# First MLP group of a hybrid decoder step: normalised a block per tile, up-projection weights in the slots free first, squares on ScalarE

## The reference, cut to what matters

```python
h   = rms_norm(x) * (1 + sc1) + sh1
proj = h @ w_in                       # q | f | i | g | B | C | h
# HGRN2 heads: gated recurrence over chunks of 64, per-head RMSNorm, SiLU gate
# short conv: y = B * causal_depthwise_conv3(C * h)
x   = x + g1 * (concat([o_rec, o_conv]) @ w_out)
h2  = rms_norm(x) * (1 + sc2) + sh2
x   = x + g2 * (square(relu(h2 @ w_up)) @ w_down)      # D_FF = 4096
y   = rms_norm(x) * g_final
```

## Time and profile before

| | |
|---|---|
| time, median of 3 runs | 898.47 us (895.25 to 898.91) |
| the profiled execution, its time | 894.26 us |
| its span on the slowest core (0) | 892.7 us |
| spans of the eight cores | 883.8 to 892.7 us |
| mean granted TensorE clock | 0.978 to 0.986 |
| TensorE, VectorE, ScalarE, GpSimd busy | 92, 54, 40, 19% |
| DMA | 106.71 MB, mean 120 GB/s |

### The profile page before, as it was taken

How to read it: one execution, slowest core, us unless ns; L and a number is a source line. 1 busy time by engine, 2 the same in 40 slices (tenths; PEclk the granted TensorE clock), 3 DMA queues, 4 the chain that set the end, 5 groups by cost and what they waited for, 6 DMA issues and landing times.

```text
span 892.7 us, 16990 instructions; the slowest of 8 cores (883.8 to 892.7 us)
## 1 busy us (share of the span) xinstructions
PE 825.2 (92%) x6005; PEld 521.0 (58%) x6005; DVE 482.7 (54%) x902; ACT 361.1 (40%) x771; POOL 173.4 (19%) x231
## 2 busy tenths in 40 slices
PE   1488899999999999876999999999999999999996
PEld 1356687677775776734544654465456545654864
DVE  1365797577777867771551764256335634542422
ACT  3266874546667666612401532233123312311412
POOL 3110134344115235200002101100210111011002
PEclk9888999999999999989999999999999999999999
DMA  8999914958995243999993513122222113102001
GB/s 154 193 193 195 200 45 98 193 171 173 205 206 139 96 142 72 189 167 173 187 210 109 194 52 115 48 95 71 95 84 71 60 48 118 36 13 89 30 2 48
DMA packets 27727, 106.71 MB, mean 120 GB/s; under 512 B 3798, under 2 KB 4822, under 8 KB 22652
## 3 DMA queue, kind: packets, MB, share of 16 engines
q0 software_dynamic: 6624, 44.14, 29.6%
q1 hardware_dynamic: 19292, 55.46, 18.3%
q10 hardware_dynamic: 1728, 6.03, 2.1%
HBM read 123.93 MB, written 22.68 MB: 164 GB/s over the span
## 4 chain that ended last, share of the span: by engine, by line
PE 81%; DMA 7%; issue 4%; DVE 4%; ACT 3%; POOL 0%; DVEq 0%; ACTq 0%; POOLq 0%; SPq 0%
PE B L484 79%; DMA xn<-x 4%; DMA xe<-xp 3%; PE B L495 2%; ACT W L511 2%; DVE W L522 1%; DMA cB<-constB 0%; DVE W L518 0%; DVE Sd L518 0%; DVE W L528 0%; ACT A L511 0%; DVE mix L518 0%; DVE hT L524 0%; DVE W L532 0%; ACT WX L511 0%
## 5 line engine op out<-in xcount | busy, mean ns | idle before, releaser
L484 PE MATMUL B<-h2T,wup 128*128 128x384 bf16 (+1 forms) x1536 | 242.2, 319 | 9.0 <-DVE uT L518 6.9
L484 PE MATMUL B<-wdn,uT 128*128 128x512 bf16 (+1 forms) x1120 | 237.5, 373 | 0.0
L511 ACT ACTIVATE W<-B 128x384 f32<-128x384 f32 (+2 forms) x241 | 119.0, 496 | 231.7 <-PE B L484 206.6
L484 PEld LDWEIGHTS B<-h2T,wup 128*128 128x128 bf16 x1536 | 150.2, 98 | 95.5 <-issue 12.2
L484 PE MATMUL B<-hT,win 128*128 128x256 bf16 (+1 forms) x1728 | 199.8, 273 | 6.5 <-DMA win<-w_in 4.8
L484 PEld LDWEIGHTS B<-hT,win 128*128 128x128 bf16 x1728 | 162.1, 100 | 32.3 <-issue 7.3
L484 PEld LDWEIGHTS B<-wdn,uT 128*128 128x128 bf16 x1120 | 109.0, 98 | 121.9
L518 DVE TENSOR_TENSOR uT<-W,B 128x384 bf16<-128x384 f32 (+1 forms) x192 | 100.5, 530 | 108.8 <-ACT W L511 87.8
L518 POOL TENSOR_TENSOR xr<-xr,W 128x512 f32<-128x512 f32 x63 | 82.6, 1312 | 284.4 <-DVE W L518 264.1
L518 DVE TENSOR_TENSOR W<-B,Gp 128x512 f32<-128x512 f32 (+1 forms) x65 | 44.0, 679 | 106.2 <-PE B L484 103.5
L484 PE MATMUL B<-wout,mix 128*128 128x512 bf16 x272 | 64.9, 390 | 9.1 <-DVE mix L518 7.0
(11 more groups left out here) (150 smaller groups left out, 643.7 us busy)
## 6 DMA issues: line engine op xcount, KB each, us to landing
x<-xr SPq DMA_DIRECT2D x17, 512.0 KB, 5.9
xn<-x SPq DMA_DIRECT2D x17, 512.0 KB, 4.4
xr<-x SPq DMA_DIRECT2D x17, 512.0 KB, 3.4
ada<-w_ada POOLq DMA_DIRECT2D x8, 1024.0 KB, 16.4
xr<-xp SPq DMA_DIRECT2D x16, 512.0 KB, 7.6
wdn<-w_down POOLq DMA_DIRECT2D x8, 1024.0 KB, 35.3
wup<-w_up POOLq DMA_DIRECT2D x8, 1024.0 KB, 22.3
yp<-xr SPq DMA_DIRECT2D x15, 512.0 KB, 2.6
```

Of the source, the lines that this page charges most:

```text
L484: ins = e.matmul(o_, lhsT=l_, rhs=r_, start=st, stop=sp_, skip_group_check=True)
L511: return P.op("act", lambda e: e.activation(out=out, in_=in_, func=func, **kw), r, w, c, prio=prio)
```

## The change

Seven things change together.

1. Group 0 is [0, 1, SAMPLE] in place of [SAMPLE, 0, 1]. Its blocks are normalised one at a time, at step H of prompt tiles 4, 5 and 6 (`n_` 5 to 7), in place of all three at step B of the last tile. h2T0 gets a layout with the block outermost (its right-hand side in `up` is three pieces of 128 columns) and moves to the place of Gs. The sample block's modulation uses its own xn buffer as scratch.
2. The class N of banks (transposes of norms) is served in the order of the code (FIFO).
3. The first two blocks of group 1 are fetched at step F of the last tile (`got`); group 1 is normalised after 12 of the 32 chains of group 0's `up`.
4. The weight slots are dealt anew: wup0 and wup1 get the region that wdn0 and wdn1 had and stand at the same place of GpSimd's queue; wup2 to 7 follow the order in which the last tile frees `win`; UPORD and upos go. wdn2 to 7 wait for the mixer's last TensorE operation.
5. In group 0's `up` both operations are on ScalarE: relu from the bank into the bank, then its square into uT. VectorE takes no part. Later groups stay as they were.
6. Gs can't be loaded before group 0's `up` has read h2T0; Gs and g_final are loaded after it. The 16 state steps, whose buffers overlap Gs, stay in group 1.
7. The prompt's conv state is stored from uc (128 pieces of 32 bytes) and no longer from uco (512 pieces of 8 bytes). Tile to mix slot follows a list, since slot 2 now overlaps h2T0.

```diff
-    FIFO = "PXU"
+    FIFO = "PXUN"
...
-    for j, off in enumerate((u0, u0 + 8192, u0 + 16384, a0 - 8192, a0 + 24576, a0 + 32768, a0 + 40960, a0 + 49152)):
+    for j, off in enumerate((4 * 8192, u0 + 16384, 7 * 8192, 8 * 8192, a0 + 24576, a0 + 32768, a0 + 40960, a0 + 49152)):
...
+    for j, off in enumerate((u0, u0 + 8192, 8192, 2 * 8192, 0, 3 * 8192, 5 * 8192, 6 * 8192)):
+        t, rg = place("wup%d" % j, [128, 8, 512], BF16, offset=off)
...
-    h2T0, _ = place("h2T0", [128, 8, 384], BF16, offset=m0)
+    h2T0, _ = place("h2T0", [128, 3, 8, 128], BF16, offset=xG + 4096)
...
-        mi = state["mixi"] % 3
+        mi = (0, 1, 2, 0, 1, 0, 2, 1, 0)[state["mixi"]]
...
+            if pre == "h2T0_":
+                act(bank[:, 0:N], bank[:, 0:N], AF.Relu, [bn], [bn])
+                act(uT[:, fc, 0:N], bank[:, 0:N], AF.Square, [bn], ["uT%d" % fc])
+                continue
             W, Wn = WB.take()
             act(W[:, 0:N], bank[:, 0:N], AF.Relu, [bn], [Wn])
-            tt("dve", uT[:, upos[fc], 0:N], W[:, 0:N], bank[:, 0:N], ALU.mult, [Wn, bn], ["uT%d" % fc])
+            tt("dve", uT[:, fc, 0:N], W[:, 0:N], bank[:, 0:N], ALU.mult, [Wn, bn], ["uT%d" % fc])
...
-    bgroups = [[SAMPLE, 0, 1], [2, 3, 4], [5, 6, 7], [8, 9, 10], [11, 12, 13], [14, 15]]
+    bgroups = [[0, 1, SAMPLE], [2, 3, 4], [5, 6, 7], [8, 9, 10], [11, 12, 13], [14, 15]]
...
+            if step == "H" and n_ in (5, 6, 7):
+                norm2(bgroups[0][n_ - 5:n_ - 4], None, "h2T0_", n_ - 5)
+            if step == "F" and n_ + 1 == len(tiles):
+                got = [fetch2(blk) for blk in bgroups[1][:2]]
             if step == "B" and n_ + 1 == len(tiles):
-                WB = View(wall[2:6])
-                for j in UPORD[:7]:
+                for j in range(2, 8):
                     load_up(j)
-                norm2(bgroups[0], h2T0, "h2T0_")
-        if n_ == 6:
-            load_dn(0); load_dn(1)
+                load_dn(0)
+                load_dn(1)
+        if n_ == 5:
+            load_up(0); load_up(1)
+    mixed = [[o for o in P.ops if o.eng == "pe"][-1]]
+    for j in range(2, 8):
+        load_dn(j, mixed)
...
+            up(bl, None, "h2T0_", 0, 12)
+            norm2(bgroups[1], h2T, "h2T", 0, got)
+            up(bl, None, "h2T0_", 12, 32)
+            load_gates(1, prompt=False)
```

More of the change, by code:

```diff
@@ L600, in assemble @@
         P.buf("wout%d" % j, rg); wout.append(t); wout_n.append("wout%d" % j)
[L601 to L604, removed]
     a0 = at["p"]
@@ L639, in assemble @@
     uT, _ = place("uT", [128, 32, 384], BF16, offset=a0)
-    for i, fc in enumerate([4 * b + i for b in UPORD for i in range(4)]):
-        P.buf("uT%d" % fc, (a0 + i * 768, a0 + (i + 1) * 768))
-    upos = {fc: i for i, fc in enumerate([4 * b + i for b in UPORD for i in range(4)])}
+    for fc in range(32):
+        P.buf("uT%d" % fc, (a0 + fc * 768, a0 + (fc + 1) * 768))
     u0 = at["p"]
@@ L680, in assemble @@
     SR = Ring("S", 2, [128, 512], F32, offset=xG + 4096)
+    h2T0, _ = place("h2T0", [128, 3, 8, 128], BF16, offset=xG + 4096)
+    for s in range(3):
+        P.buf("h2T0_%d" % s, (xG + 4096 + s * 2048, xG + 6144 + s * 2048))
     xeR = Ring("xe", 2, [128, 1024], F32, offset=xG)
-    SbF = (one("rout", [128, 512], F32, offset=xG + 4096), "rout")
+    SbF = (one("rout", [128, 512], F32, offset=xG + 8192 + 2048), "rout")
     sg2R = Ring("sx", 2, [128, 512], F32, offset=xG + 4096)
@@ L736, in load_up, with load_dn @@
         dma("pool", flat(wup[j]), wup_d[j], [], [wup_n[j]], MB2)
-    def load_dn(j):
-        dma("pool", flat(wdn[j]), wdn_d[j], [], [wdn_n[j]], MB2)
+    def load_dn(j, after=()):
+        dma("pool", flat(wdn[j]), wdn_d[j], [], [wdn_n[j]], MB2, after=after)
     P.buf("cBm", P.bufs["cB"].rng, "cB")
@@ L1123, in mixer_tile @@
                    [csn, nH], [ubn])
[L1124 to L1127, removed]
+                copy("pool", uc[:, ccs[0]:ccs[0] + 2, :], uv[:, :, 256:258], [ubn], [ucn])
                 for i, cc in enumerate(ccs):
@@ L1179, in mixer_tile, with fetch2, norm2 @@
             dma("sp", x1_d[xblk + b], xr[:], [xrn], ["x1_%d" % (xblk + b)], 128 * 4096)
-    def norm2(blocks, h2T, pre):
-        for s, blk in enumerate(blocks):
-            nbv, nbn = normed(None, None, fetch(x1_d[blk], ["x1_%d" % blk], None, "sp"))
+    def fetch2(blk):
+        return fetch(x1_d[blk], ["x1_%d" % blk], None, "sp")
+    def norm2(blocks, h2T, pre, s0=0, got=()):
+        for i, blk in enumerate(blocks):
+            s = s0 + i
+            x = got[i] if i < len(got) else fetch2(blk)
+            nbv, nbn = normed(None, None, x)
+            dst = h2T0[:, s, :, :] if pre == "h2T0_" else h2T[:, :, s * 128:(s + 1) * 128]
             if blk == SAMPLE:
-                sample_mod(nbv, nbn, h2T, pre + "%d" % s, s * 128, 16, 24)
+                sample_mod(nbv, nbn, dst, pre + "%d" % s, 0, 16, 24, x)
                 continue
@@ L1228, in part @@
             bank, bn = banks[(s, dh)]
-            mm([(bank[:, :], uT[:, upos[a * 8 + k], s * 128:(s + 1) * 128], wdn[dh * 4 + a][:, k, :], a == 0 and k == 0, a == 3 and k == 7)
+            mm([(bank[:, :], uT[:, a * 8 + k, s * 128:(s + 1) * 128], wdn[dh * 4 + a][:, k, :], a == 0 and k == 0, a == 3 and k == 7)
                 for k in range(8)], ["uT%d" % (a * 8 + k) for k in range(8)] + [wdn_n[dh * 4 + a]], [bn])
@@ L1258, in finish @@
                 for a in range(4):
-                    mm([(bank[:, 0:c1 - c0], uT[:, upos[a * 8 + k], s * 128:(s + 1) * 128], wdn[dh * 4 + a][:, k, h0:h0 + c1 - c0],
+                    mm([(bank[:, 0:c1 - c0], uT[:, a * 8 + k, s * 128:(s + 1) * 128], wdn[dh * 4 + a][:, k, h0:h0 + c1 - c0],
                          a == 0 and k == 0, a == 3 and k == 7) for k in range(8)],
```

49 lines of the change are left out of this document (26 added, 23 removed).

## The result

The changed kernel took 884.14 us (median of four runs, 883.08 to 886.49), the kernel before 898.47 us beside it. The ratio is 0.9853, with a 95% interval of 0.9832 to 0.9875: 13.2 us faster by the ratio and 14.3 by the medians, where 16.4 were forecast. One more set of runs on another chip gave 886.28 us and a ratio of 0.9828 (0.9798 to 0.9858). Now and then an execution is some per cent longer at a lower clock on some cores; the medians here leave such slow runs out, as the ratios do.

What follows compares the result with a forecast made beforehand. The prediction took TensorE, busy 92% of the span, as the bound. Gaps and slow clock of 19.4 us less costs of 2, 0, 1 and 0 gave 16.4 us, so 882 us from a median of 898.47; range 875 to 893 us.

Steps and rivals of the forecast that it cites:

- The gaps and the slow clock: End of mixer and first up-projection: three TensorE gaps, 14.6 us, and slow clock, 2.45 and 2.3 us, all gained.
- the first two gaps: TensorE waits before the last tile's output projection, 5.59 us, and before the first up-projection, 2.19 us; both would go.
- the third: TensorE gap of 6.86 us in the middle of the first up-projection, traced to a late xn load; would go.
- Term (1): Normalising the first group in prompt tiles 4 to 6 costs the mixer 2 us, bounds minus 2 to 15.7.
- Rival D: Mixer, 280 to 350 us: ScalarE stands on late next-tile x loads, five waits of 5.7 us; 910 us; chance 0.07.
- Term (2): First up-projection: ScalarE's relu and square take 1.0 to 1.15 us a pair, TensorE stays the bound; cost 0.
- Term (3): Weight loads on POOL's queue: last lands near 463 us, TensorE asks at 463.9; level, cost 1 us.
- Term (4): Gs, loadable only after h2T0 is read, lands near 458 us; cover 17 us, cost 0, up to +3.
- wup0 at the projection: Sign of being right: wup0's matmuls begin within 1 us of the last hT projection, near 377 us.
- the first up without a gap: Sign of being right: the first group's up-projection has no gap of over 1 us.
- Clock 1.00 in each window from 250 us: Sign of being right: granted clock 1.00 in every 10 us window from 250 us to the last.
- The first down chains 16 to 20 us earlier: Sign of being right: the end of the first down chains comes 16 to 20 us earlier.

Runs made afterwards that it cites:

- e4: Changed kernel with the whole norm of the first MLP group back behind the mixer, before the first up chain: 894.70 us, ratio 0.9952.
- e5: Changed kernel with the second group's norm behind the whole first up-projection; its early loads, meant to go, stayed where they were: 890.14 us, ratio 0.9877.
- e1: Changed kernel with the first group's three norms later, at steps H of tile 6 and G and H of tile 7: 888.45 us, ratio 0.9899.
- g1: Changed kernel with the first of the norms' x1 loads on ScalarE's DMA queue in place of SyncE's: 883.80 us, ratio 0.9837.
- e2: Changed kernel with the first norm's x1 load left out and all its arithmetic kept: 882.56 us, ratio 0.9819.
- e3: Changed kernel with the first group's up-projection squares back on VectorE: 882.67 us, ratio 0.9825.
- k5_actswapvec: Changed kernel with first x1 load on ScalarE's queue, wdn6 ahead of wdn7, and first group's squares on VectorE again: 878.83 us, ratio 0.9747.
- k1_swap: Changed kernel with the last two weight loads swapped on GpSimd's queue, wdn6 ahead of wdn7: 879.76 us, ratio 0.9788.
- after: The changed kernel itself, as first measured against the kernel before: 884.14 us, ratio 0.9853.
- a0_after: The changed kernel, unchanged, run on another chip for comparison: 886.28 us, ratio 0.9828 to the kernel before.
- f1: Changed kernel with one 1 MB weight load fewer, wdn1 not loaded and its chains reading wdn0: 877.91 us, ratio 0.9766.

## Why the prediction was right, and where its steps were off

**The gaps and the slow clock, 19.4 us: right.** On core 0 the span fell by 20.7 us: 19.4, and 2.0 for wup0 that begins earlier than the transposes had ended, less 1.15 of wait for wdn, leaves 0.4 unexplained. (The 376.9 us that I called the end of the last projection are the end of the 16 transposes behind it; the sum doesn't change by that, since the same work is done at both points, but for 8 more transposes now.) e4 shows the step behind the first two gaps: with the norms back behind the mixer both return. For the third, no run brought it back: in e5 no square stood between the relus, and the loads stayed early. That it came from the late xn rests on the earlier trace rows and on its absence after.

**Term (1), the mixer, 2 us: the mis-sized term.** From the end of those transposes before to the start of wup0 now, the four cores without a stop moved by -2.0, -1.0, -1.6 and +2.3 us (cores 0, 2, 5, 7). The others, with stops of 3 to 11 us, moved by 8.3, 4.3, 6.4 and 3.6 us (cores 1, 3, 4, 6), and the time is the slowest core's. I priced the norms as work, between minus 2 and 15.7 us, and looked at 270 to 370 us. The x1 load that they bring was counted nowhere in that term. Rival D had the mechanism, ScalarE in order in front of a late xn with the state chain behind it, but with the wrong place (280 to 350 us), five times over, and with xn<-xp, which was the late load only where an edit had moved things (e1, e4, g1). e2 shows that with this load gone the stop is gone on all cores. The row to open was the DMA share from 220 us on, here in the kernel before on core 0:

```profile
230.00:240.00 10.00, 10.00 (x69) 6.28 (x67) 7.89 (x16) 8.47 (x18) 1.53 (x6) 1.00 1.00 214
240.00:250.00 10.00, 8.72 (x83) 6.66 (x83) 4.50 (x8) 7.36 (x16) 1.22 (x2) 1.00 1.04 213
```

**Term (2), ScalarE's pair: right.** 0.96 us against the 1.0 to 1.15 forecast, and TensorE was never released by uT; e3 and k5_actswapvec put its cost and its worth at nothing.

**Term (3), the weights, 1 us: right in kind, too small.** The rates held: 115.5 us from first issue to last landing as a mean, and on core 0 the last landed at 462.3 where I had 463. But I took the order of the last two loads as that in which they are asked for, and it isn't: wdn6 lands last and is asked for first. The wait was 1.2 to 4.3 us on seven cores, and k1_swap, in which it is gone, is 4.4 us faster. It was also no fixed date, as I had it, but hangs on the mixer's progress, so that it adds to term (1).
The rule that I weighed there, the Trainium skill's "DMA: Bandwidth & Descriptors", section "Anatomy of one DMA — SWDGE (gpsimd) path", gave an estimate of 6.8 us a load. This trace disagrees: 14 loads in 114.9 us on core 4 are 8.2 us each, with SyncE's transfers beside them.

**Term (4), Gs: wrong date, right cost.** It was issued at 435.3 us and took 39.4 us; it landed at 474.7, not near 458, and VectorE stood on it for 15.5 us. TensorE was never released by it in the changed kernel. But the cover is used up: in k1_swap on core 4, where the waits for wdn are gone, VectorE stood on Gs for 17.8 us, ScalarE 39.2 us on GpSimd's sum behind it, and TensorE then waited 2.52 us for uT at 475 us. With the weights in time, this is the next limit there.

**The signs named in advance.** wup0 at the projection, the first up without a gap: seen. Clock 1.00 in each window from 250 us: not seen on core 4 (0.53 and 0.50 from 250 to 260). The first down chains 16 to 20 us earlier: by the first vS matmul behind them 20.8 us on core 0 (494.86 to 474.03) and 9.6 on core 4 (494.01 to 484.37). The forecast was near in part by luck. A gain 1.3 us larger than computed on the undisturbed cores met a loss that falls on four of eight. And the profiled execution fell from 894.26 to 883.94 us, by 10.3 us, where the sum has 16.4; what brought the forecast near was that the profiled execution before had been 4.2 us under its median, and the one after lies at its median.

## What to carry to other kernels

A step that is moved takes its load with it: look at the DMA share and the queue where the load will be issued, not only at the engines where the work will stand, and ask which in-order engine will stand in front of it. Where a chain of loads starts on a signal from the stage before, a stop in that stage makes the loads late as well, and the two waits lie in a row. Taking one away need not give its length back: without the stop the loads here took longer, and the wait behind it grew. Read every core, since a loss on some of them sets the time.

## What was unexpected of the hardware

- The landing of one 512 KB load has two values in the same program: 14.4 us on core 0 and 31.2 on core 4, both with a DMA share of 1.0. Which cores are hit changes between executions (1, 3, 4, 6, then 0, 3, 5, 7), but never both of the pairs 0 and 1, 2 and 3, 4 and 5, 6 and 7: in none of the 14 profiled executions, the kernel before included, did TensorE stop on both cores of a pair there. In the six in which the load stands on SyncE's queue (after, a0_after, e3, e5, f1, k1), 23 of 24 pairs have one core at 20.3 to 31.2 us and the other at 13.9 to 15.7. So the cores share no data, but they aren't independent of each other; what a pair shares, and what decides which of the two is late, stays open.
- The queue on which a load is issued moves its landing, though the DMA engines are full either way: on the four late cores of the changed kernel 23.3 to 31.2 us behind two stores on SyncE's queue, and 15.3 to 16.4 us for the load issued 1 us later on ScalarE's; on the other four 14.4 to 15.6 and 11.4 to 13.2. Moved to ScalarE's queue (g1), the x1 took 12.2 to 16.2 us. The Trainium skill ("DMA: Bandwidth & Descriptors", section "Issuing engines are not separate DMA queues") says that another issuing engine saves issue time only; that doesn't hold here. The same page's section "Queues, rings and completion order" says that each DMA engine takes turns between the queues that have work for it, and with that this trace agrees.
- An ACTIVATE of 384 elements that reads and writes PSUM took 475 ns, one from PSUM to SBUF 489 ns.
